# A two-layer diffusion backbone on one core: fp32 products of the opening's filter transforms and of layer 1's attention done in three fp32r passes, with the splits that this needs

## The reference, cut to what matters

```python
# layer 0, upper half of the width: Hyena, whose filters are made from a small MLP
h = sin(f1 * (z @ w1 + b1)); h = sin(f2 * (h @ w2 + b2)); h = h @ w3      # (L, order 2, 2, 1024)
h = h * exp(-t * deltas)
k = concat(h[:, 0], 0, h[:0:-1, 1]);  k = k / sum(abs(k))
y = irfft(rfft(u) * rfft(k))          # plus bias * u
# layer 1: dense GQA (8 heads, 2 kv heads) and MLA (8 heads; key = 128 nope + 64 rope)
s = einsum('qd,kd->qk', q, k) * dk ** -0.5;  o = softmax(s) @ v
```

## Time and profile before

| | |
|---|---|
| runs | 1462.16, 1463.1, 1463.9 us; median 1463.1 |
| the profiled execution | 1461.12 us, of which the span is 1459.3 |
| PE | 1416.9 us busy (97%), 7032 matmul records |
| DVE, ACT, POOL | 1005.1 (69%), 549.9 (38%), 270.4 us (19%) |
| granted TensorE clock, mean | 0.994 |
| DMA | 273.25 MB; the opening at 339 to 387 GB/s, later mostly 150 to 200 |

### The profile page before, as it was taken

How to read it: one execution, slowest core, us unless ns; L and a number is a source line. 1 busy time by engine, 2 the same in 40 slices (tenths; PEclk the granted TensorE clock), 3 DMA queues, 4 the chain that set the end, 5 groups by cost and what they waited for, 6 DMA issues and landing times.

```text
span 1459.3 us, 17711 instructions
## 1 busy us (share of the span) xinstructions
PE 1416.9 (97%) x7032; PEld 1124.7 (77%) x7032; DVE 1005.1 (69%) x1212; ACT 549.9 (38%) x782; POOL 270.4 (19%) x289
## 2 busy tenths in 40 slices
PE   4999999999999999999999999998999999999998
PEld 1335888888888878777888788888878777888887
DVE  3394999999999777786877555456445666555454
ACT  2554222222222333443333411125436555555432
POOL 1000543344443000000002144443000111000000
PEclk9999999999999999999999999999999999999999
DMA  9998556554655654445455766751334342332574
GB/s 349 387 369 339 176 165 210 159 204 157 202 161 166 205 185 146 152 155 195 157 191 210 286 204 233 235 164 66 130 118 146 129 156 88 116 115 88 187 248 142
DMA packets 63218, 273.25 MB, mean 187 GB/s; under 512 B 6736, under 2 KB 13088, under 8 KB 43296
## 3 DMA queue, kind: packets, MB, share of 16 engines
q1 hardware_dynamic: 42960, 194.51, 38.0%
q0 software_dynamic: 20176, 77.61, 16.4%
HBM read 257.40 MB, written 14.69 MB: 186 GB/s over the span
## 4 chain that ended last, share of the span: by engine, by line
PE 89%; DVE 4%; DMA 4%; ACT 2%; issue 1%; POOL 0%; SPq 0%; DVEq 0%; ACTq 0%
PE banks L1051 18%; PE banks L1052 17%; PE banks L1055 17%; DMA ada_ring<-in_ada_first 3%; PE banks L2141 2%; PE banks L2142 2%; PE banks L2147 2%; PE banks L1953 2%; PE banks L1956 2%; PE banks L1959 2%; PE banks L1256 2%; PE banks L2304 2%; PE banks L2176 2%; PE banks L1336 1%; PE banks L563 1%
## 5 line engine op out<-in xcount | busy, mean ns | idle before, releaser
L1051 PE MATMUL banks<-xh,wh 128*128 128x512 f32 (+1 forms) x1296 | 479.2, 378 | 0.0
L1052 PE MATMUL banks<-xl,wh 128*128 128x512 f32 (+1 forms) x1296 | 467.2, 369 | 0.0
L1013 DVE TENSOR_TENSOR wl<-raw,wh 128x2048 fp32r<-128x2048 f32 (+1 forms) x125 | 282.7, 2262 | 106.2 <-ACT wh L1007 106.1
L1007 ACT ACTIVATE wh<-raw 128x2048 fp32r<-128x2048 f32 (+1 forms) x125 | 236.8, 1895 | 238.3 <-PE banks L1055 126.2
L1051 PEld LDWEIGHTS banks<-xh,wh 128*128 128x128 f32 x1296 | 244.2, 188 | 49.3 <-issue 9.1
L1055 PE MATMUL banks<-xh,wl 128*128 128x512 f32 (+1 forms) x1296 | 279.7, 368 | 0.0
L1052 PEld LDWEIGHTS banks<-xl,wh 128*128 128x128 f32 x1296 | 244.4, 189 | 43.0 <-issue 3.6
L1055 PEld LDWEIGHTS banks<-xh,wl 128*128 128x128 f32 x1296 | 227.1, 189 | 40.5
L398 DVE SCALAR_TENSOR_TENSOR ada_acc<-ada_w,cond,ada_acc 128x1024 f32<-128x1024 f32 x120 | 168.0, 1400 | 4.1 <-DMA ada_w<-in_ada_rest 2.0
L421 POOL DMA_DIRECT2D ada_w<-in_ada_rest x128 | 69.4, 542 | 508.0 <-DVE ada_acc L410 336.6
L410 DVE SCALAR_TENSOR_TENSOR ada_acc<-ada_w,cond,ada_acc 128x1024 f32<-128x1024 f32 x90 | 131.5, 1461 | 0.0
(11 more groups left out here) (348 smaller groups left out, 1890.7 us busy)
## 6 DMA issues: line engine op xcount, KB each, us to landing
ada_w<-in_ada_rest POOLq DMA_DIRECT2D x128, 512.0 KB, 4.1
raw<-in_ev_tiles SPq DMA_DIRECT2D x52, 1024.0 KB, 6.2
ada_ring<-in_ada_first SPq DMA_DIRECT2D x32, 1024.0 KB, 11.9
raw<-in_out_tiles SPq DMA_DIRECT2D x16, 1024.0 KB, 7.2
raw<-in_od_wide SPq DMA_DIRECT2D x16, 1024.0 KB, 4.9
raw<-in_od_gates SPq DMA_DIRECT2D x16, 1024.0 KB, 4.9
raw<-in_out_wide SPq DMA_DIRECT2D x16, 1024.0 KB, 5.8
hT<-in_hT POOLq DMA_DIRECT2D x4, 1024.0 KB, 10.5
```

Source lines behind the costliest of these rows:

```text
L1007: nc.scalar.activation(b.wh[:, t % 2, 0:width], b.raw[:, t % 2, 0:width], ACT.Copy).then_inc(s.hi_done, 1)
L1013: nc.vector.tensor_tensor(b.wl[:, t % 2, 0:width], b.raw[:, t % 2, 0:width], b.wh[:, t % 2, 0:width].bitcast(F32), ALU.subtract).then_inc( ...
L1051: nc.tensor.matmul(out, wh[:, k, :], b.xh[:, seg, k, :], start=(k == 0), stop=False)
L1052: nc.tensor.matmul(out, wh[:, k, :], b.xl[:, seg, k, :], start=False, stop=False)
```

## The change

**Opening.** The lag matrix is split once (three ACT copies, three POOL subtractions) and for each filter `flt_d` and `flt_s` into `dif_high`, `sum_high` (ACT) and `dif_low`, `sum_low` (POOL). PE does three passes through the new `lag_products`: lag_high·high, lag_low·high, then, behind a wait for POOL's low, lag_high·low. The 8 fp32 matmuls of a filter become 24 fp32r. The first row, which the sum needs with the tap added, is remade by DVE from both parts in five operations in place of two. The lows lie where `flt_s` and `flt_d` lay, the highs over `flt`.

**Layer 1's attention.** Scores 2 fp32 matmuls to 6 fp32r, outputs 4 to 12. ACT makes highs of keys, queries and values, POOL their lows (per MLA unit 128x512, 128x256 and 128x512; per GQA unit the queries' 128x256 alone; kgqa and vgqa once, 128x1024 each), DVE the lows of the probabilities (`prob_lows`). The MLA rope part stays fp32. POOL's last token rotation moves to slot 25. The gate row's load moves from slot 32 to behind the last outputs, on SP's queue behind the first two raw tiles of the last block.

**Smaller.** vtok ahead of the drain, and one semaphore for all four ztok copies; O rows in 12 slots and eleven loads early, raw tile 1 ahead of the twelfth; the norm's tile split behind k = 1; low passes of `up_keys` and `up_queries` moved behind the wait for `lo_done`. Semaphores are merged and renamed.

```diff
-O_SLOT = (0, 1, 2, 3, 4, 5, 0, 1, 2, 6, 3, 4, 5, 0, 1, 2)
+O_SLOT = (0, 1, 2, 3, 4, 5, 7, 8, 9, 10, 11, 6, 0, 1, 2, 3)
-        for n in range(9, KT):
-            if n == 10:
+        for n in range(11, KT):
+            if n == 12:
                 load_raw(sp, b, s, t0 + 1, out_weights(g, 1), (KT, P))
-NORM_SPLIT = {9: 2, 13: 3, 15: 4}
+NORM_SPLIT = {1: 1, 9: 2, 13: 3, 15: 4}
...
+        def lag_products(high, low, parts, bank, count):
+            for m in parts:
+                for h in range(2):
+                    nc.tensor.matmul(ps[bank + m // 2], lag_high(b, h, m), high[:, h, :], start=(h == 0), stop=False)
+                    nc.tensor.matmul(ps[bank + m // 2], b.lag_low[:, h, m * P:(m + 1) * P], high[:, h, :], start=False,
+                                     stop=False)
+            pe.wait_ge(s.parts_low, count)
+            for m in parts:
+                for h in range(2):
+                    last = nc.tensor.matmul(ps[bank + m // 2], lag_high(b, h, m), low[:, h, :], start=False, stop=(h == 1))
+                last.then_inc(s.k_mm, 1)
...
             if stage == 3:
                 pe.wait_ge(s.flt_sd, 3 * f + 3)
+                lag_products(b.sum_high, b.sum_low, (0, 2), 4, filter_lows(f, 2))
...
+                act.wait_ge(s.flt_abs, 4 * f + 4)
+                act.wait_ge(s.flt_sd, 3 * f + 2)
+                a.activation(b.dif_high[:], b.flt_d[:], ACT.Copy).then_inc(s.parts_high, 1)
+                a.activation(b.sum_high[:], b.flt_s[:], ACT.Copy).then_inc(s.parts_high, 1)
...
-                chain(v.tensor_tensor(b.tap[:], ps[5][0:1, :], b.hybias[:], ALU.mult))
-                dve.wait_ge(s.flt_sd, 3 * f + 2)
-                v.tensor_tensor(b.flt_s[0:1, 0, :], b.flt_s[0:1, 0, :], b.tap[:], ALU.add).then_inc(s.flt_sd, 1)
+                chain(v.tensor_tensor(b.hybias[:], ps[5][0:1, :], b.hybias[:], ALU.mult))
+                dve.wait_ge(s.parts_low, filter_lows(f, 2))
+                row_high, row_low = b.sum_high[0:1, 0, :], b.sum_low[0:1, 0, :]
+                chain(v.tensor_tensor(b.hybias[:], b.hybias[:], row_low.bitcast(F32), ALU.add))
+                chain(v.tensor_tensor(b.hybias[:], b.hybias[:], row_high.bitcast(F32), ALU.add))
+                chain(v.tensor_copy(row_high, b.hybias[:]))
+                v.tensor_tensor(row_low, b.hybias[:], row_high.bitcast(F32), ALU.subtract).then_inc(s.flt_sd, 1)
...
+            pe.wait_ge(s.kq_low, kq_splits(j))
+                nc.tensor.matmul(ps[2 + r], qh[:, rows], kh, start=True, stop=False)
+                nc.tensor.matmul(ps[2 + r], qh[:, rows], kl, start=False, stop=False)
+                last = nc.tensor.matmul(ps[2 + r], ql[:, rows], kh, start=False, stop=(u < 8))
...
+            pe.wait_ge(s.v_low, v_splits(j))
+                nc.tensor.matmul(ps[6][:, 0:256], vh[:, k, :], b.probT1[:, k, :], start=(k == 0), stop=False)
+                nc.tensor.matmul(ps[6][:, 0:256], vl[:, k, :], b.probT1[:, k, :], start=False, stop=False)
+            pe.wait_ge(s.p_low, j + 1)
+                last = nc.tensor.matmul(ps[6][:, 0:256], vh[:, k, :], b.probl1[:, k, :], start=False, stop=(k == 3))
...
+        sp.wait_ge(s.h_out, 80)
+        sp.wait_ge(s.pv_mm, L0_UNITS + KT)
+        sp.dma_start(b.grow[:], g.gate_d.to_broadcast((P, D))).then_inc(s.spread_in, 16)
```

More of the change, by code:

```diff
@@ L252, in sbuf_map @@
     b.flt_d = put("flt_d", "HL", 20 * K, [P, 2, 512])
+    b.sum_low = put("sum_low", "HL", 16 * K, [P, 2, 512], F32R)
+    b.dif_low = put("dif_low", "HL", 20 * K, [P, 2, 512], F32R)
+    b.sum_high = put("sum_high", "U", 56 * K, [P, 2, 512], F32R)
+    b.dif_high = put("dif_high", "U", 60 * K, [P, 2, 512], F32R)
     b.flt_abs = put("flt_abs", "HL", 24 * K, [P, 4, 512])
@@ L537, in _ @@
             pool.dma_start(b.hT[:, 4 * q:4 * q + 4, :], g.hT[:, 4 * q:4 * q + 4, :]).then_inc(s.x_in, 16)
+        for n, (h, first, end) in enumerate(LAG_PARTS):
+            pool.wait_ge(s.parts_high, 2 + n + 1)
+            part = b.lag[:, h, P * first:P * end]
+            nc.gpsimd.tensor_tensor(b.lag_low[:, h, P * first:P * end], part, b.lag_high[n][:].bitcast(F32),
+                                    ALU.subtract).then_inc(s.parts_low, 1)
         for f in range(4):
             o, c = f // 2, f % 2
+            pool.wait_ge(s.parts_high, filter_highs(f, 1))
+            nc.gpsimd.tensor_tensor(b.dif_low[:], b.flt_d[:], b.dif_high[:].bitcast(F32), ALU.subtract).then_inc(s.parts_low, 1)
+            pool.wait_ge(s.parts_high, filter_highs(f, 2))
+            nc.gpsimd.tensor_tensor(b.sum_low[:], b.flt_s[:], b.sum_high[:].bitcast(F32), ALU.subtract).then_inc(s.parts_low, 1)
             if f < 3:
@@ L1159, in _ @@
             if i == L0_TILES:
-                for n in range(9):
+                for n in range(11):
                     load_o(sp, b, s, g, n)
@@ L1489, in _ @@
                     s.vtok_ready, 1)
+            drain(i)
+            if i == 1:
+                act.wait_ge(s.core_in, 80)
+                a.activation(b.fwdh[:], b.fwd[:], ACT.Copy).then_inc(s.parts_high, 1)
+            if hyena_job(i, 4, 1) is not None:
+                odd_halves(hyena_job(i, 4, 1))
+            if hyena_job(i, 2, 5) is not None:
+                ztok(hyena_job(i, 2, 5))
             if 0 <= kv < KV and r == 2:
@@ L2286, in prob_transposes @@
                 pe.wait_ge(s.probT_ready, L0_UNITS + j)
+                pe.wait_ge(s.p_low, j)
             else:
@@ L2686, in _ @@
                 rotate("q0")
+            if l1_unit(i - 1) is not None:
+                prob_lows(l1_unit(i - 1))
             if l1_unit(i) is not None:
```

259 lines of the change are left out of this document (173 added, 86 removed).

## The result

| | before | after |
|---|---|---|
| median of the runs (4 and 4) | 1463.5 us | 1477.68 us (1477.49 to 1478.17) |
| ratio, 95% interval | | 1.0099 [1.0084, 1.0114] |
| the profiled execution, its span | 1461.12, 1459.3 | 1477.69, 1475.8 |
| PE busy, mean granted clock | 1416.9 (97%), 0.994 | 1414.6 (96%), 0.985 |

What follows compares the result with a forecast made beforehand. PE, busy 97% of the span, was taken as the bound. Terms 13.0 - 10.2 - 1.2 - 1.7 - 0.9 - 0.9 - 0.3 + 0.5 = -1.7 gave a median of 1461.4 us, range 1452 to 1470.

Steps and rivals of the forecast that it cites:

- the opening: Added waits at the four filters plus clock falls, less a ring wait: +13.0 us, ends 0 and +23.
- DVE's four end at 45.7: Filter 0: DVE's four row operations follow sum_low at 43.2 and end at 45.7, within that filter's +3.3 us.
- rival 1: Opening: POOL is dear, 1.73 us per 512-column subtraction beside DVE; +6.3, net +4.6, 1467.7 us; chance 0.16.
- rival 4: MLA slots of layer 1's attention: DVE and POOL block each other, reductions come late; net +4.9, 1468.0 us; chance 0.10.
- Filter 2: Opening, third filter: DVE's row ends at 85.2 instead of 82.2, delaying x's splits, nu, kstage and arow: +3.0 us.
- The clock: Opening: PE falls to low clock behind a 6.3 us gap and, counted half, a 3.2 us gap: +3.0, ends 0 and +10.
- Rival 2: Opening: the clock falls in all four filters, 10 us in place of 3.0; net +5.3, 1468.4 us; chance 0.10.
- The *end: End of the opening: the last ring wait, 1.38 us, goes because later requests find an emptier queue: -1.4 us.
- The attention: Layer 1, sixteen units: cheaper scores and outputs save 0.35 + 0.29 us each, -10.2 us; range -7 to -10.6.
- O rows: Eleven of sixteen loads go out early and raw tile 1 leaves earlier: -1.7 us of a 2.4 wait, 0 to -3.5.
- norm: Second tile's wl moved behind x's second piece, so PE waits less for the reciprocal: -1.2 us; 0 or -3 otherwise.
- Query rows: PE starts 3.2 us earlier but meets the next wl instead: -0.3 us, to -3.2.

Runs made afterwards that it cites:

- the first run: Changed kernel with the opening as before (lag matrix unsplit, fp32 transforms), everything else as changed: 1456.05 us, ratio 0.9954.
- Experiment 3: Changed kernel with POOL's dif_low and sum_low subtractions halved: 1474.84 us; or instead with DVE's small operations behind filter 0's and 2's rows: 1472.63 us.
- Experiment 2: Changed kernel with ACT copying sabs and arow ahead of the filters' highs in the opening: 1468.35 us, ratio 1.0042.
- experiment 4: Changed kernel with unread matmuls in three PE waits: 12 ahead of stage 3 of filters 0 and 2, 26 ahead of filter 1's arow; 1473.72 us.
- mended opening: Changed kernel with sabs and arow ahead of highs, DVE's small operations behind rows, 12 unread matmuls ahead of stage 3 of filters 0 and 2: 1465.95 us.

## Why the prediction was wrong

**The sign of the whole** hung on the opening, put at +13.0 with ends 0 and +23. It came out at +21.1 by the profile and 21.6 by the first run. The range gave that end too little: the dear POOL and every fall of the clock together would have reached it (by my own prices 13.0 + 6.3 + 7.0 = 26.3, and not the 23 that I wrote), but I had priced them as rivals, one at a time. POOL was not dear, so that sum would have been right by luck. Three steps of it failed.

- *"DVE's four end at 45.7."* They end at 46.96, 1.3 late. The prices were right (0.68, 0.68, 0.41, 0.68), and so was sum_low's end. The step took DVE to be free at 43.2, with the row's product made long before. I had looked at what DVE's operations do to POOL (rival 1) and not at what POOL's run of seven microseconds does to DVE's small ones. I had used that rule for the MLA slots, in rival 4, and not where POOL was put to work beside DVE for the first time. Experiment 3 puts 5.2 us on it in the opening, most of it in filter 2.
- *"Filter 2: ... on them ACT's nu, behind those kstage and the next arow: +3.0."* It was +6.1. The highs stand on ACT ahead of sabs in filters 2 and 3 as well, and PE waits 1.89 and 2.39 for sabs before it can turn the sums. In the forecast the highs ahead of arow and sabs counted only at filters 0 and 1. In filter 2 DVE's small operations were shut out too (2.28 and 2.32), and behind them stood a scaling of x. Experiment 2 puts 8.2 on ACT's order, over all four filters.
- *"The clock: +3.0 ... by my sum a gap of 6.3 (falls) and one of 3.2 (I take half)."* Both fell, and filter 2 as well. The opening lost 5.9 us more of PE's work than before, twice my term. Rival 2's mechanism was real in three of its four filters, and not confined to the opening. The price of a fall was right at filter 0 (2.2 us by experiment 4, 2.5 by the missing share of the clock) and too high at filters 1 and 2 (1.5 and 1.7). The Trainium skill ("TensorE: Matmul & The Clock Gate", on how clock oscillation bites in kernels), which I had used for that rival, tells of bursts that each start at the low clock behind a wait. The trace agrees at filters 0, 1 and 2, behind gaps of 3.77, 6.37 and 4.01. Filter 3's gap of 2.39 is shorter than the waits of which that page tells, so its full clock does not speak against the page: that by its rule every new gap pays was my reading, and it went too far.

The *end*, -1.4 forecast, was +1.4: the wait for the ring is gone as said, and one of 1.68 for arow stands in its place. A wait that goes because PE is late is replaced by whatever the lateness leaves behind; I had asked that of the attention and not here.

**Right in the opening:** the largest wait (6.3 forecast, 6.37), the wait ahead of stage 3 (3.2, 3.77), POOL's durations, and that PE's savings hide in waits. Filter 1 with its clock came out as summed, 2.1 + 1.8 = 3.9.

**The attention**, -10.2 with -7 to -10.6 about it, gave -7.6. The term was right in size per slot (0.63 for 0.64). The loss in the first units is of the kind named; POOL's vl beside wl is the row for it.

**O rows**, -1.7 with 0 to -3.5, was +2.4 together with vtok. The step that failed was to count a merged semaphore as no change. The wait that row 0 now has is for a later row, and the clock falls twice, 1.7 each, where it fell once before. The run with separate semaphores has one wait of 2.6 and no fall, and the two versions that differ in the semaphores alone are 5.8 us apart. The *norm's* 1.2 came (1.7 to 0.6), and a clock stretch behind it that is 1.7 longer took it back. That stretch is as long (3.8) in the version with opening, O rows and norm as before, and short (2.3) in the first run, which has the move, so the move is not its cause.

**Key rows** right (-0.9 forecast, -1.1). **Query rows** by the profile +0.2, by the run that takes the move back -1.9, with intervals that overlap: in the changed kernel the wait moves to L2376 (2.18, on ACT's qo) and takes the clock along; where the move is undone, the clock falls behind the 3.2, which it did not in the kernel before. **Gate row** right in sign: the last block has +1.1 for +0.5, and no run takes the move back.

**The row.** Of the remaining 10.8 us of a mended opening 7.5 belong to the row that is remade, part directly (the wait for POOL's last low and four operations in series) and part by the clock behind it. So of what a mended opening still costs it is the largest term. Without it three passes still cost 3.3 more than fp32 there. Open is how the rest divides between POOL's pair in series and ACT.

## What to carry to other kernels

Splitting an fp32 product into three fp32r passes pays where the splits are made a slot ahead on engines with slack (0.63 us for each unit here), and costs where the same engines stand between PE and its next input: the passes of the opening saved about 5 us of PE's work at full clock (0.6 for each of eight groups, where I had 0.7 to 0.8), and the opening ended 21 later. Ask of each added instruction what stands behind it in its queue, and of each operation of DVE what POOL does beside it, small ones above all. A wait that counts merged semaphores waits for the latest of them. And price every new gap of PE of about 2 us or more with a chance of a fall of the clock, which costs 1.5 to 2.5 us of work, wherever it lies.
